# GpSimd in place of VectorE for the four weight sums of the cross-attention's query product

## The reference, cut to what matters

```python
for l in range(DEPTH):                                   # DEPTH = 2
    h = rms_norm(x, norm_mix[l])
    ...                                                  # recurrent heads and dilated attention
    x = x + jnp.concatenate([y_hg, y_att], axis=-1) @ w_out[l]
    x = x + memory_cross_attention(rms_norm(x, norm_cross[l]), rms_norm(mem, norm_mem[l]),
                                   wq_x[l], wkv_x[l], wo_x[l])
    x = x + hierarchical_moe(rms_norm(x, norm_ffn[l]), ...)
return rms_norm(x, norm_final)

def memory_cross_attention(h, mem_n, wq, wkv, wo):
    q = (h @ wq).reshape(B, S, X_HEADS, X_DH)            # the product that the change touches
    ...                                                  # scores against 256 memory tokens, softmax, values
    return o.astype(h.dtype) @ wo
```

## Time and profile before

| | us |
|---|---|
| median of three runs | 990.96 |
| lowest and highest | 990.73, 994.08 |
| span of the profiled execution | 991.6 |
| PE busy | 970.2 (98%) |
| PE's weight loads busy | 526.7 (53%) |
| DVE busy | 511.3 (52%) |
| ACT busy | 148.9 (15%) |
| POOL busy | 134.5 (14%) |

### The profile page before, as it was taken

How to read it: one execution, slowest core, us unless ns; L and a number is a source line. 1 busy time by engine, 2 the same in 40 slices (tenths; PEclk the granted TensorE clock), 3 DMA queues, 4 the chain that set the end, 5 groups by cost and what they waited for, 6 DMA issues and landing times.

```text
span 991.6 us, 12328 instructions
## 1 busy us (share of the span) xinstructions
PE 970.2 (98%) x4989; PEld 526.7 (53%) x4996; DVE 511.3 (52%) x890; ACT 148.9 (15%) x348; POOL 134.5 (14%) x131
## 2 busy tenths in 40 slices
PE   8999999999999999999999999999999999999996
PEld 7668445669575453333334954465974433333332
DVE  2523486766553435443554567686656533334333
ACT  3202000411011111111112100042020111011112
POOL 3066132000010000000001943210000100000000
PEclk9999999999999999999999999999999999999999
DMA  9963301963379999999999260077397899999994
GB/s 357 425 242 131 131 1 37 391 254 125 130 291 383 417 424 418 421 423 420 421 419 422 109 254 1 2 312 281 128 358 278 339 421 419 421 421 420 421 413 164
DMA packets 45119, 293.65 MB, mean 296 GB/s; under 512 B 5504, under 2 KB 5760, under 8 KB 13312
## 3 DMA queue, kind: packets, MB, share of 16 engines
q1 hardware_dynamic: 38288, 266.36, 66.1%
q10 hardware_dynamic: 5616, 22.24, 5.7%
q0 software_dynamic: 1152, 4.19, 1.1%
HBM read 283.33 MB, written 9.44 MB: 295 GB/s over the span
## 4 chain that ended last, share of the span: by engine, by line
PE 94%; DMA 2%; DVE 1%; POOL 1%; issue 1%; ACT 0%; POOLq 0%; DVEq 0%; SPq 0%; ACTq 0%
PE bank L1073 21%; PE bank L1153 11%; PE bank L616 9%; PE bank L634 6%; PE bank L846 6%; PE bank L636 6%; PE bank L708 5%; PE bank L900 5%; PE bank L964 5%; PE bank L736 5%; PE bank L1112 3%; PE bank L606 2%; PE bank L1107 2%; PE bank L772 2%; PE bank L918 1%; PE bank L934 1%
## 5 line engine op out<-in xcount | busy, mean ns | idle before, releaser
L1073 PE MATMUL bank<-ring,hT 128*64 128x512 f32 x704 | 181.3, 593 | 0.0
L1073 PEld LDWEIGHTS bank<-ring,hT 128*64 128x64 f32 x704 | 58.2, 137 | 92.3 <-issue 92.3
L616 PE MATMUL bank<-ring,hT 128*128 128x512 f32 x192 | 85.6, 599 | 0.0
L2091 DVE TENSOR_TENSOR x<-bank,x 128x512 f32<-128x512 f32 x64 | 43.3, 692 | 46.0 <-PE bank L1112 46.0
L1479 POOL TENSOR_TENSOR sm<-sm 128x1 f32<-128x1 f32 x4 | 1.0, 239 | 449.5 <-ACT both L1271 241.5
L616 PEld LDWEIGHTS bank<-ring,hT 128*128 128x128 f32 x192 | 35.5, 190 | 40.7 <-issue 40.2
L1153 PE MATMUL bank<-ring,xs 128*64 128x512 f32 x224 | 56.7, 595 | 0.0
L846 PE MATMUL bank<-ring,hT 128*128 128x512 f32 x128 | 56.3, 595 | 0.1
L1153 PE MATMUL bank<-ring,og 128*64 128x512 f32 x128 | 42.5, 595 | 0.0
L1073 PE MATMUL bank<-work,hT 128*64 128x512 f32 x96 | 42.2, 593 | 0.0
L1509 POOL TENSOR_TENSOR ring<-ring 128x2048 f32<-128x2048 f32 x8 | 36.8, 4599 | 29.1 <-DMA ring<-in_w_mix 19.4
(11 more groups left out here) (325 smaller groups left out, 1660.8 us busy)
## 6 DMA issues: line engine op xcount, KB each, us to landing
ring<-in_w_experts SPq DMA_DIRECT2D x140, 1024.0 KB, 17.1
ring<-in_w_mix SPq DMA_DIRECT2D x60, 1024.0 KB, 15.8
work<-in_w_experts SPq DMA_DIRECT2D x20, 1024.0 KB, 15.0
late<-in_w_mix ACTq DMA_DIRECT2D x4, 2048.0 KB, 9.8
late<-in_w_experts SPq DMA_DIRECT2D x8, 1024.0 KB, 14.9
keys<-in_w_experts SPq DMA_DIRECT2D x8, 1024.0 KB, 16.8
both<-in_w_experts SPq DMA_DIRECT2D x8, 1024.0 KB, 21.4
ring<-in_w_experts SPq DMA_DIRECT2D x10, 512.0 KB, 16.3
```

Source lines behind the costliest of these rows:

```text
L616: last = nc.tensor.matmul(b[:, :], lhs[:, c, m * P:(m + 1) * P], w[:, c, :], start=(c == 0), stop=(c == C - 1))
L1073: last = nc.tensor.matmul(banks[2 + g][b2 * CAP:(b2 + 1) * CAP, :], rows_T_of(p)[:, c, b2 * CAP:(b2 + 1) * CAP], w, start=(c == 0), stop=( ...
L2091: V.tensor_tensor(xv, banks[OUT_BANK[n][m]][:, :], xv, ALU.add).then_inc(r_added[L], 1)
```

## The change

GpSimd does the four weight sums of the query product in place of VectorE. Sums 1, 2 and 3 stand in GpSimd's program between the roots of the recurrent heads' norm and `norm(1)`, behind waits for the four halves of q0 and q1; sum 4 stands behind `norm(1)` and a wait for q_1. VectorE waits for sum 4 before its own first weight sum of the product p, because both use one slot. TensorE's, ScalarE's and SyncE's programs are the same.

```diff
@@ gpsimd @@
                     root(hrs[:, m, :], hss[:, m, :], P, HG_HEADS).then_inc(hrs_done, 1)
+                def q_weights(i, dst, one, two):
+                    minus(dst, one, two, ALU.subtract).then_inc(q_weight_sum, 1)
+                    pool.wait_ge(q_weight_sum, 4 * L + i)
+
+                q11, q21, q12, q22 = (weight_block(L, name, k) for name in ("q1", "q0") for k in range(2))
+                qt1, qt2 = weight_block(L, Q_SUMS, 0), weight_block(L, Q_SUMS, 1)
+                for name in ("q0", "q1"):
+                    for half in range(2):
+                        wait_loaded(pool, L, name, half)
+                wait_free(pool, L, Q_SUMS)
+                q_weights(1, qt1, q12, q11)
+                q_weights(2, qt2, q22, qt1)
+                q_weights(3, q12, q22, q12)
                 norm(1)
+                wait_job(pool, L, "q_1")
+                q_weights(4, q11, q21, qt2)
                 norm(2)
@@ vector @@
-                def q_weights(i, dst, one, two):
-                    V.tensor_tensor(dst, one, two, ALU.subtract).then_inc(q_weight_sum, 1)
-                    dve.wait_ge(q_weight_sum, 4 * L + i)
-                for name in ("q0", "q1"):
-                    for half in range(2):
-                        wait_loaded(dve, L, name, half)
-                wait_free(dve, L, Q_SUMS)
-                q_weights(1, qt1, q12, q11)
-                q_weights(2, qt2, q22, qt1)
                 add_out(0, 0)
-                q_weights(3, q12, q22, q12)
                 add_out(1, 0)
...
                 q_sum("q_2", 0, 1, "q_1")
-                q_weights(4, q11, q21, qt2)
                 for name in ("p0", "p1"):
                     for half in range(2):
                         wait_loaded(dve, L, name, half)
                 wait_free(dve, L, P_SUMS)
+                dve.wait_ge(q_weight_sum, 4 * L + 4)
                 p_weights(1, pt1, p12, p11)
```

More of the change, by code:

```diff
@@ L1874, in _ @@
                 emptied(V.tensor_copy(hT[:, 4:6, :], bank("ap0")[:, :].rearrange("p (a t) -> p a t", t=T)))
-                q11, q21, q12, q22 = (weight_block(L, name, k) for name in ("q1", "q0") for k in range(2))
-                qt1, qt2 = weight_block(L, Q_SUMS, 0), weight_block(L, Q_SUMS, 1)
                 p11, p21, p12, p22 = (weight_block(L, name, k) for name in ("p0", "p1") for k in range(2))
                 pt1, pt2 = weight_block(L, P_SUMS, 0), weight_block(L, P_SUMS, 1)
-                def q_weights(i, dst, one, two):
-                    V.tensor_tensor(dst, one, two, ALU.subtract).then_inc(q_weight_sum, 1)
-                    dve.wait_ge(q_weight_sum, 4 * L + i)
                 def p_weights(i, dst, one, two):
```

## The result

The changed kernel takes 1018.61 us (median of four runs, 1018.25 to 1022.44) against 991.89 us of the kernel before on the same chip: 26.7 us more, a ratio of 1.0276 with a 95% interval of 1.0257 to 1.0296. The forecast was 1013.9 us, 22.9 us more, in a range of 1003 to 1019: the time lies at the upper edge of it. Of the 4.7 us between the two times 3.8 are in the difference, and 0.9 come from the kernel before, whose median rose from 990.96 to 991.89 with a fourth run.

The account below looks back on a forecast made before the run. TensorE was taken to bound the kernel, with 94% of the chain. Shares 16.2, token sums 3.3 and slow clock 3.4 us sum to 22.9 us over 990.96, giving 1013.9 us, range 1003 to 1019.

Parts of the forecast that it names:

- step 1: Attention softmax: VectorE's shares wait for GpSimd's sums 1 to 3, so TensorE's values start late; 16.2 us over both layers.
- step 3: Behind TensorE's stop at the shares: its clock drops to the 1.2 GHz level, 1.7 us a layer, 3.4 us.
- What is removed is worth nothing: VectorE's four weight sums per layer: taking them off gains 0, since VectorE was waiting for TensorE anyway.
- the sign that I named: In the profile after, TensorE's idle time names VectorE's share line twice, with about 8 us.
- Step 2: Token sums ahead of q_6: VectorE's first waits for GpSimd's sum 4, 1.65 us a layer, 3.3 us in all.
- A: At the softmax shares: they aren't held off, only the token sums cost 3.3 us; 994.3 us; chance 0.09.
- B: At the softmax shares: VectorE gets more turns than GpSimd, shares 4 and 5 both slip in; say 1004 us; chance 0.10.
- C: At the shares and behind: a fourth turn or a longer slow stretch of the clock; 1019 us and more; chance 0.06.
- D: On VectorE: the change is a gain because its 9 us a layer come off the path; chance 0.02.

Follow-up runs that it names:

- all sums late: Changed kernel, but sums 1 to 3 also wait for share 5 and sum 4 for token sum 4; 991.63 us against 992.21, ratio 0.9996.
- both edits: Changed kernel with softmax part 2's transposes repeated eighteen times to fill TensorE's stop, and part 0's copy ahead of share 4; 1012.09 us against 991.37.

## Where the prediction was right, and which of its steps fell short

The direction, the mechanism and both places were right. What failed is the size, in two terms of the sum: step 1, the shares, put at 16.2 us and measured at 18.1, and step 3, the clock, put at 3.4 us and measured at 4.8. Together they are 3.3 of the 3.8 us that the difference is larger than forecast. Term by term:

- **What is removed is worth nothing:** held. The kernel with all sums late is as fast as that of before (0.9996, 0.998 to 1.0012).
- **Step 1, the shares, 16.2 us:** this is the larger miss. It held in its turns, with 4.8 us for a share that waits a whole turn, and was 1.9 us short. TensorE's transposes of parts 4 and 5, due at 194.75 and 687.5 by the rows before them, came at 203.26 and 697.10: 8.5 and 9.6 us, 18.1 in place of 16.2. Two things were missing. Part 4's transposes go into the bank that part 0 was in, and that bank is emptied by a copy behind share 5. So the sign that I named, TensorE's wait on VectorE's share line, did not come: the waits name the copies. I let them start at share 5's end and only the values wait for copies, 0.2 us a layer. The experiment with the copy first moved the stop's end from the copy to the share, 0.7 us a layer. And in layer 1 the weights landed 1.05 us later against TensorE's work than in the profile before: sum 1 starts 1.77 us behind the wo row at 679.71, where the landing stood 0.7 us behind it before. I had written that the landing counts one for one, but gave it no width. It has one: in seven profiles with the sums or the zeros at that place (the changed kernel, and those with sums 1 to 3 alone, with zeros, in halves, kept busy, with the copy first, and with both edits) the first stands between 0.5 and 2.0 us behind that wo row.
- **Step 2, the token sums, 3.3 us:** exact. q_6 comes 1.65 us later, and the kernel with sum 4 alone shows 1.77 us in layer 0.
- **Step 3, the clock, 3.4 us:** right in kind and short by 1.4 us. It measured 3.0 + 1.8 = 4.8 us in the profile, and keeping TensorE busy brought 5.1 us on the medians. I took the length of the slow stretch behind the router, 3.4 us, as that of any slow stretch. It is 10.2 us in both layers of the changed kernel, of which 6.1 and 3.8 us lie behind the stop, where TensorE has work.
- **The sum against the span:** 18.1 + 4.8 + 3.3 is 26.2, and the median moved by 26.7. The two spans differ by 24.8 only. The runs that have both show a span 1.8 to 2.0 us under the time, so the profiled execution of before, with a span of 991.6, was itself some 2.5 us over the median of 990.96, not 0.6 as I wrote. Its layer 1 had the slow stretch behind the router, which costs 1.0 us against the profile of the late sums; the changed kernel's profile has it too, from 793 on. What only the profile of before has is a wait of 0.78 us for a transfer right behind the experts' first products:

```profile
789.62 1.09 PE L1097 MATMUL bank<-ident,xs 128*128 128x128 f32 x8 [0.78 <-DMA xs<-by_slot]
```

  With that, and some 0.6 us at the start and the end, 26.2 us become the 24.8 of the spans. It changed the base and not the difference that I forecast.
- **Rivals:** A, that a share isn't held off for its small second operand, is out with 4.7 to 4.8 us. B, that VectorE gets more turns, is out for this kernel, but its reason wasn't empty: with the issue 0.06 us the other way, a share does slip in. Of C the fourth turn did not occur, but its other half did: the slow stretch was longer than I counted, and the time ended 0.4 us short of the 1019 from which C was to begin. That it ended inside the range is luck to that extent. D did not occur.

## What to carry to other kernels

Work moved to a half idle engine is free only where it doesn't hold off another engine's instructions: before GpSimd gets SBUF-reading sums, list VectorE's instructions with two SBUF inputs that fall into their time and ask which of them TensorE waits for. The price is the number of such instructions that come behind a running sum, times what one sum lasts, so halving the instruction takes more than half of the price away here (10.6 in place of 26.7 us), and a wait that places the sums after the last of them removes it. A stop of TensorE also costs behind its end: count the slow stretch as a term with a width.

## What the runs showed of the hardware

- A VectorE share of 0.69 us stands still for the whole remainder of a GpSimd subtraction and lasts up to 4.8 us, and isn't slowed at all beside GpSimd's writes of zeros (0.692 us over twelve shares). The page "SBUF — State Buffer" of the Trainium skill, section "Who interferes with whom", says both, and the runs agree: two SBUF inputs count against a GpSimd instruction that reads, not against one that only writes.
- A second input of two values a row, broadcast over 256, counts as a whole one. Before, the rows had shown it for equal inputs, and for a broadcast input only that it holds GpSimd off.
- The order is decided by the issue, at a lead of 0.06 us, in both layers of the kernel that waits for share 3. A sum that a semaphore releases starts 0.18 us after the share that releases it; VectorE's next share stands 0.12 us after the same one.
- Behind stops of 8.35 and 9.41 us TensorE's slow stretch went on for 6.1 us in one layer and 3.8 in the other, the whole stretch being 10.2 us in both. It followed stops of 1.79 and 3.27 us too (the sums in halves), and not those of 1.40 us (sum 1 behind share 3), nor waits of 1.11 and 1.87 us with TensorE kept busy ahead of them.
